# Moving one modulation piece of the feed-forward loop from ahead of the residual additions to behind the second one

## The chip, the cores and the metric

The kernel runs on one core of a Trainium2 chip. The metric is the time of one execution on the device in microseconds (us): the median of three runs, and less is better. Beside it there is one profiled execution, whose span and rows are read below.

The engines of the core are named as in the profile: PE (TensorE matmul), PEld (TensorE weight load), DVE (VectorE), ACT (ScalarE), POOL (GpSimd) and SP (SyncE, which here issues the loads of weights).

## The reference, cut to what matters

Two transformer blocks run one after the other on 1024 tokens of width 1024. The change lies in the feed-forward part of the first block, under which the kernel also computes the modulation vectors of the second block, since these depend only on the input `c`:

```python
h = _rmsnorm(x, norm_ffn[l])
gate, up = jnp.split(h @ w_gu[l], 2, axis=-1)          # 1024 x 2*2816
x = x + (jax.nn.silu(gate) * up) @ w_down[l]           # end of the first block
...
c_act = jax.nn.silu(c)                                 # one vector of 1024
shift, scale, gate = jnp.split(c_act @ ada_w[l] + ada_b[l], 3, axis=-1)   # for l = 0, 1
shift, scale = jnp.split(c_act @ kv_ada_w + kv_ada_b, 2, axis=-1)
```

Together the modulation is the product of one vector of 1024 with a matrix of 1024 x 8192. The kernel takes it in eight groups of 1024 columns, one group in each of eight passes of the loop, and each group in eight pieces of 128 rows.

## The kernel before, in words

**The hidden tiles.** The hidden width of 2816 is 22 tiles of 128. The first two are made before the loop, the others in ten steps `i` of two tiles: `i` = 0 stands alone and has no modulation, `i` = 1 to 8 are the passes of a hardware loop, each with one group of the modulation, and `i` = 9 stands alone behind it. A pass does three things on PE, in this order:

- `quad(i, 0, GATE_AT)`: the gate product of two new tiles, in seven products ("forms") of sums of weights with sums of activations (Strassen's scheme), 12 matmuls each;
- `down(i)`: the previous two hidden tiles (`act_hi`, `act_lo`) times the down weights, in eight output tiles `o` = 0 to 7, 12 matmuls each. Tile `o` goes to `pair(2 + o % 2)`, so only two PSUM pairs (banks 4 and 5, banks 6 and 7) take turns. From `o` = 2 on, tile `o` may start only when the residual addition of tile `o - 2` has read its pair;
- `quad(i, 1, UP_AT)`: the up product, seven forms again. The form with index 3 is the product's fourth.

The wait of `down(i)` in PE's queue is

```python
pe.wait_ge(ffn_res, 8 * i + (o - 1))
```

where `ffn_res` counts the residual additions, eight to a pass.

Each product is taken in a high and a low part (fp32r), which is why every piece gives matmuls at lines 691, 692 and 694 of the helper `product`.

**DVE** works through one program in order. In a pass that is `ada_add(i, 0)`, `gate_first`, `ada_add(i, 1)`, `gate_tiles` (additions of the gate product's forms, and at lines 3073 and 3077 the multiplication of `gated` by `rms3`), `ada_add(i, 2)`, and then the eight residual additions (line 3122, `xT` plus a PSUM pair), among which stand `gate_scale` (line 3082, behind `o` = 0 and `o` = 2) and pieces 3 to 6 of the modulation, behind `o` = 1, 3, 5 and 7. Piece 7 and `ada_turn` (a transpose and a reduction, lines 3005 and 3007) follow, and then `up_tiles`, which begins at line 3088 with reading bank 3.

**One piece of the modulation**, `ada_add(i, k)`, waits for its 128 x 1024 block of the matrix in `ada_raw[:, k % 2]` and adds its product with column `k` of `cact` to `ada_acc` (line 2998; the first piece, line 2995, writes it). Both of its large operands lie in SBUF.

**SP** issues every load in one queue. `load_ada(i, k)` (line 1275) waits for piece `k - 2`, since the pieces take turns in two buffers:

```python
sp.wait_ge(ada_summed, 8 * i + (k - 9))
```

Loads 0, 1 and 2 are queued ahead of `after_quad(i, GATE_AT, 2)`, load 3 behind it, and loads 4 to 7 behind `after_down(i, DOWN_AT, 4)`. These two issue halves of weight strips (line 1348), as soon as a form made from the half before is ready. What is queued behind load 7 is the first weight half of the next pass, which waits for the form with index 3 of the up product.

**POOL and ACT** make the forms of the weights: ACT writes the high part (line 2486), POOL the low part (line 1548) and the sums (lines 1559, 1561, 1564 and 1566), all from operands in SBUF. PE's form with index 3 of the up product needs POOL's chain 1548, 1564, 1566, 1548, of which the first starts when `down` has given back its last weights.

Of the kernel before, what the change touches and what calls it, by code (L numbers as in the profile page):

```python
# [132 lines left out]
def build(nc, dram, out):  # L133
    ctx = ExitStack()
    with ctx:
# [39 lines left out]
        def col(name, i=0, n=1):  # L175
# [7 lines left out]
        chk_stack, chk_khi, chk_klo = shared([("chk_stack", [P, HEADS, T], F32R), ("chk_khi", [P, HEADS, T], F32R),  # L183
                                              ("chk_klo", [P, HEADS, T], F32R)])
        _, p1, pt1 = shared([("mla_qkv", [P, 3 * HEADS, T], F32), ("p1", [P, 4, HALF], F32), ("pt1", [P, 4, HALF], F32)])
        h_hi, h_lo = sb("h_hi", [P, NK, T], F32R), sb("h_lo", [P, NK, T], F32R)

        mraw, kv_hi, kv_lo = shared([("mraw", [P, 6, T], F32), ("kv_hi", [P, T], F32R), ("kv_lo", [P, T], F32R)])
        _, swa_klo0, swa_bias, p3, pt3 = shared([("x_kept", [P, KEPT, T], F32), ("swa_klo0", [P, T], F32R),
                                                ("swa_bias", [P, SWA_HEADS, 2 * P], F32), ("p3", [P, 4, 2 * P], F32),  # L190
                                    ("pt3", [P, 4, 2 * P], F32)])
        fox_rows, = shared([("fox_rows", [P, QT, D], F32R)])
        _, memw_lo = shared([("w18", [P, 6, T], F32), ("memw_lo", [P, 2, 8, P], F32R)])
        _, p_lo_x = shared([("w20", [P, 6, T], F32), ("p_lo_x", [P, 2, T], F32R)])
        xT = sb("xT", [P, NK, T])
# [67 lines left out]
        def pair(p):  # L263

            return ps[:, 2 * p * HALF:2 * (p + 1) * HALF]
# [87 lines left out]
        def form_through(eng, i, p):  # L353
            eng.wait_ge(form_done, FORMS * i + p + 1)
# [2414 lines left out]
        def _(dve):  # L2769
# [220 lines left out]
            def ada_add(i, k):  # L2990

                r = k % 2
                dve.wait_ge(ada_loaded[r], 16 * (4 * i + (k // 2 - 3)))
                if k == 0:
                    dve.tensor_scalar(ada_acc[:, :], ada_raw[:, r, :], cact[:, 0:1], None, ALU.mult).then_inc(ada_summed, 1)
                else:
                    dve.wait_ge(ada_summed, 8 * i + (k - 8))
                    dve.scalar_tensor_tensor(out=ada_acc[:, :], in0=ada_raw[:, r, :], scalar=cact[:, k:k + 1],  # L2998
                                             in1=ada_acc[:, :], op0=ALU.mult, op1=ALU.add).then_inc(ada_summed, 1)

            def ada_turn(i):


                dve.wait_ge(ada_summed, 8 * i)
                dve.transpose(ada_turned, ada_acc[:, :]).then_inc(ada_turns, 1)
                dve.wait_ge(ada_turns, i)
                dve.tensor_reduce(ada_part[:, :], ada_turned.rearrange("p (b c) -> p b c", c=STREAM), AX.X, ALU.add)\
                   .then_inc(ada_parts, 1)

            def ada_columns(i):  # L3010
                dve.wait_ge(ada_cols, i)
                for q in range(P // STREAM):
                    r = slice(q * STREAM, (q + 1) * STREAM)
                    dve.tensor_tensor(adav[r, bass.ds(i * 8 - 8, 8)],
                                      bank(7, D // STREAM)[r, :].rearrange("p (t q) -> p q t", q=P // STREAM)[:, q, :],
                                      cols[r, bass.ds(i * 8 + (COLS["adab"] - 8), 8)], ALU.add).then_inc(ada_read, 1)
# [3 lines left out]
            def hidden_low(n, j, hi, lo):  # L3020

                dve.wait_ge(ffn_hi, HID * n + (j + 1))
                dve.tensor_tensor(lo[:, j, :], gated[:, j, :], rows(hi[:, j, :]), ALU.subtract).then_inc(ffn_lo, 1)
# [35 lines left out]
            def gate_first(i, at):  # L3059
                form_through(dve, i, at + 1)  # L3060
                dve.wait_ge(quad_first, 2 * i + 1)
                dve.wait_ge(ffn_lo, HID * i + HID)
                dve.tensor_tensor(gated[:, 0, t1], one_sum, bank(3), ALU.add).then_inc(quad_read, 1)

            def gate_tiles(i, at):
                two_products(i, 0, at)
                more_products(i, 0, at)
                dve.tensor_tensor(gated[:, 1, t2], three_sum, bank(2), ALU.add).then_inc(quad_read, 1)
                form_through(dve, i, at + 5)
                read_through(i, 0, 4)  # L3070
                dve.tensor_tensor(gated[:, 0, t2], two_sum, bank(3), ALU.add).then_inc(quad_read, 1)
                read_through(i, 0, 6)
                dve.tensor_tensor(gated[:, 0, :], gated[:, 0, :], rms3[:, :], ALU.mult).then_inc(ffn_gate, 1)
                form_through(dve, i, at + 6)
                dve.tensor_tensor(gated[:, 1, t1], three_sum, bank(1), ALU.add).then_inc(quad_read, 1)
                read_through(i, 0, 7)
                dve.tensor_tensor(gated[:, 1, :], gated[:, 1, :], rms3[:, :], ALU.mult).then_inc(ffn_gate, 1)

            def gate_scale(i, j):

                dve.wait_ge(ffn_silu, HID * i + (HID + j + 1))
                dve.tensor_tensor(gated[:, j, :], gated[:, j, :], rms3[:, :], ALU.mult).then_inc(ffn_mul, 1)

            def up_tiles(i, at):
                dve.wait_ge(ffn_mul, 2 * HID * i + 2 * HID)
                form_through(dve, i, at + 1)
                dve.wait_ge(quad_first, 2 * i + 2)
                dve.tensor_tensor(three_sum, one_sum, bank(3), ALU.add).then_inc(quad_read, 1)
                read_through(i, 1, 1)
                dve.tensor_tensor(gated[:, 0, t1], gated[:, 0, t1], three_sum, ALU.mult).then_inc(ffn_mul, 1)  # L3090
                two_products(i, 1, at)
                dve.wait_ge(ffn_mul, 2 * HID * i + 2 * HID + 1)
                more_products(i, 1, at)
                dve.tensor_tensor(one_sum, three_sum, bank(2), ALU.add).then_inc(quad_read, 1)
                read_through(i, 1, 5)
                dve.tensor_tensor(gated[:, 1, t2], gated[:, 1, t2], one_sum, ALU.mult).then_inc(ffn_mul, 1)
                form_through(dve, i, at + 5)
                dve.tensor_tensor(two_sum, two_sum, bank(3), ALU.add).then_inc(quad_read, 1)
                read_through(i, 1, 6)
                dve.tensor_tensor(gated[:, 0, t2], gated[:, 0, t2], two_sum, ALU.mult).then_inc(ffn_done, 1)  # L3100
                form_through(dve, i, at + 6)
                dve.tensor_tensor(three_sum, three_sum, bank(1), ALU.add).then_inc(quad_read, 1)
                read_through(i, 1, 7)
                dve.tensor_tensor(gated[:, 1, t1], gated[:, 1, t1], three_sum, ALU.mult).then_inc(ffn_done, 1)

            def ffn_pair(i, ada):
                if ada:
                    ada_add(i, 0)
                gate_first(i, GATE_AT)
                if ada:  # L3110
                    ada_add(i, 1)
                gate_tiles(i, GATE_AT)
                if ada:
                    ada_add(i, 2)
                for o in range(8):
                    if o % 2:
                        form_through(dve, i, DOWN_AT + o // 2)
                    else:
                        dve.wait_ge(ffn_tile, 4 * i + (o // 2 + 1))
                    if not isinstance(i, int):  # L3120
                        dve.wait_ge(ffn_res, 8 * i + (o - 7))
                    dve.tensor_tensor(xT[:, o, :], xT[:, o, :], pair(2 + o % 2), ALU.add).then_inc(ffn_res, 1)  # L3122
                    if o in (0, 2):
                        gate_scale(i, o // 2)
                    if ada and o % 2:
                        ada_add(i, 3 + o // 2)
                if ada:
                    ada_add(i, 7)
                    ada_turn(i)
                up_tiles(i, UP_AT)  # L3130
                if ada:
                    ada_columns(i)
                for j in range(HID):
                    hidden_low(i + 1, j, act_hi, act_lo)

            ffn_pair(0, False)
            with dve.Fori(1, FFN_ITERS - 1) as i:
                ffn_pair(i, True)
# [288 lines left out]
            for part, tok in enumerate(out_tokens):  # L3427
                for j in range(6 if part else NK):
                    i = NK * part + j
# [200 lines left out]
```

## Time and profile before

| | |
|---|---|
| median of 3 runs (lowest to highest) | 2430.15 us (2428.74 to 2436.74) |
| the profiled execution's own time | 2434.64 us |
| its span | 2432.8 us |
| PE busy | 2369.6 us, 97% |
| DVE busy | 1508.2 us, 62% |
| POOL busy | 1272.2 us, 52% |
| ACT busy | 833.1 us, 34% |
| mean granted clock of TensorE | 0.994 of full speed |

The profiled execution's time is its span and 1.8 us around it. It lies 4.5 us above the median of the runs. The eight passes of the loop lie between 812 and 1306 us of the span. Rows give the start and the duration in us from the span's start; a duration of a matmul is longer than the distance to the next, since matmuls are pipelined.

### The profile page before, as it was taken

The page shows a single profiled execution, that of the slowest core. Times are in us where ns is not written, and L with a number is a line of the kernel's source. Part 1 is how long each engine was busy: PE and PEld are TensorE (multiplying, and loading weights), DVE is VectorE, ACT ScalarE, POOL GpSimd, SP SyncE. Part 2 cuts the span into 40 slices and gives each one's busy share as a digit, 9 for nine tenths or more (in the row PEclk, how much of TensorE's full clock was granted, in tenths as well). Part 3 has the DMA queues.
Part 4 walks back from the last instruction along what each step waited for, and adds up shares of the span by engine and source line. Part 5 has one row for each costly group of instructions (what it writes and reads, how often), then busy time and mean ns, then how long its engine had stood idle before and what let it go on. Part 6 is the DMA issues. An engine that isn't in the chain of part 4 may idle for free.

```text
span 2432.8 us, 32824 instructions
## 1 busy us (share of the span) xinstructions
PE 2369.6 (97%) x11802; PEld 1967.0 (81%) x11810; DVE 1508.2 (62%) x1909; ACT 833.1 (34%) x1588; POOL 1272.2 (52%) x724
## 2 busy tenths in 40 slices
PE   7999999999999999999999999999999999999998
PEld 6887788888877888888888878878788787888887
DVE  6725555634577787877787678763754766045555
ACT  4211545612433222222222433231232333055663
POOL 4433964144144666666668344673746633465523
PEclk9999999999999999999999999999999999999999
DMA  6511000021011333333331111111221113100023
GB/s 213 160 44 44 1 1 27 10 113 44 18 40 48 113 121 121 121 121 121 121 121 65 48 44 44 56 66 52 69 82 56 56 65 130 52 27 19 27 104 131
DMA packets 67270, 177.31 MB, mean 73 GB/s; under 512 B 6846, under 2 KB 13760, under 8 KB 65112
## 3 DMA queue, kind: packets, MB, share of 16 engines
q1 hardware_dynamic: 58344, 148.58, 17.9%
q10 hardware_dynamic: 8816, 27.25, 3.2%
q8 instruction: 70, 1.15, 0.2%
q14 instruction: 40, 0.33, 0.0%
HBM read 160.04 MB, written 15.72 MB: 72 GB/s over the span
## 4 chain that ended last, share of the span: by engine, by line
PE 84%; DVE 7%; issue 4%; POOL 3%; ACT 2%; DMA 0%; SPq 0%; DVEq 0%; POOLq 0%; ACTq 0%
PE ps L691 22%; PE ps L692 22%; PE ps L694 22%; PE ps L843 6%; PE ps L821 5%; PE ps L831 3%; POOL split_lo L1597 1%; DVE h_lo L565 1%; DVE trail L3218 1%; PE ps L704 1%; PE ps L706 1%; PE ps L705 1%; PE ps L487 1%; DVE h_lo L568 1%; ACT p L971 0%
## 5 line engine op out<-in xcount | busy, mean ns | idle before, releaser
L691 PE MATMUL ps<-h_hi,split_hi 128*128 128x512 f32 (+1 forms) x1576 | 629.6, 399 | 20.5 <-DVE h_lo L568 13.8
L692 PE MATMUL ps<-h_lo,split_hi 128*128 128x512 f32 (+1 forms) x1576 | 613.5, 389 | 0.0
L694 PE MATMUL ps<-h_hi,split_lo 128*128 128x512 f32 (+1 forms) x1576 | 548.3, 389 | 0.0
L1473 POOL TENSOR_TENSOR split_hi<-raw,cf 128x1024 fp32r<-128x1024 f32 x70 | 136.9, 1955 | 496.9 <-PE ps L694 389.5
L691 PEld LDWEIGHTS ps<-h_hi,split_hi 128*128 128x128 f32 x1576 | 298.4, 189 | 81.3 <-issue 12.8
L694 PEld LDWEIGHTS ps<-h_hi,split_lo 128*128 128x128 f32 x1576 | 297.6, 189 | 62.0
L692 PEld LDWEIGHTS ps<-h_lo,split_hi 128*128 128x128 f32 x1576 | 298.5, 189 | 56.0 <-issue 1.2
L1548 POOL TENSOR_TENSOR split_lo<-raw,split_hi 128x512 fp32r<-128x512 f32 x144 | 231.2, 1624 | 201.5 <-ACT split_hi L2486 201.3
L1597 POOL TENSOR_TENSOR split_lo<-raw,split_hi 128x512 fp32r<-128x512 f32 x96 | 147.6, 1546 | 171.9 <-ACT split_hi L2644 171.7
L1475 POOL TENSOR_TENSOR split_lo<-raw,split_hi 128x1024 fp32r<-128x1024 f32 x70 | 195.3, 2789 | 5.5
L2486 ACT CAST split_hi<-raw 128x512 fp32r<-128x512 f32 x144 | 86.6, 622 | 287.0 <-PE ps L694 212.9
L879 DVE CUSTOM_DVE_ANT_0 p<-ps,swa_bias 128x256 f32<-128x256 f32 (+1 forms) x128 | 52.1, 407 | 154.2 <-PE ps L821 152.8
L979 ACT COPY pt<-ps 128x256 f32<-128x256 f32 (+3 forms) x216 | 79.8, 369 | 177.9 <-PE ps L831 177.0
L691 PE MATMUL ps<-act_hi,split_hi 128*128 128x512 f32 x320 | 125.5, 392 | 5.5 <-DVE xT L3122 5.5
L831 PE MATMUL ps<-cf,p 128*128 128x128 f32 x712 | 122.4, 277 | 7.6 <-ACT p L971 6.8
L692 PE MATMUL ps<-act_lo,split_hi 128*128 128x512 f32 x320 | 124.6, 390 | 0.0
L2644 ACT CAST split_hi<-raw 128x512 fp32r<-128x512 f32 x96 | 58.7, 621 | 162.2 <-PE ps L694 157.1
L831 PEld LDWEIGHTS ps<-cf,p 128*128 128x128 f32 x712 | 87.3, 145 | 29.0 <-ACT p L971 15.5
L3122 DVE TENSOR_TENSOR xT<-xT,ps 128x1024 f32<-128x1024 f32 x72 | 87.4, 1214 | 31.2 <-PE ps L694 31.2
L2998 DVE SCALAR_TENSOR_TENSOR ada_acc<-ada_raw,cact,ada_acc 128x1024 f32<-128x1024 f32 x56 | 103.6, 1850 | 0.8
L691 PE MATMUL ps<-p_hi,split_hi 128*128 128x512 f32 x256 | 100.1, 391 | 1.3 <-DVE p_lo L3202 1.3
L692 PE MATMUL ps<-y_lo,split_hi 128*128 128x512 f32 x256 | 99.6, 389 | 0.0
(447 smaller groups left out, 5136.4 us busy)
## 6 DMA issues: line engine op xcount, KB each, us to landing
raw<-in_strips SPq DMA_DIRECT2D x208, 256.0 KB, 2.7
raw<-in_strips SPq DMA_DIRECT2D x86, 512.0 KB, 3.5
ada_raw<-in_ada SPq DMA_DIRECT2D x64, 512.0 KB, 3.9
memw_raw<-in_mem_strips SPq DMA_DIRECT2D x8, 512.0 KB, 6.5
xT<-in_xT ACTq DMA_DIRECT2D x4, 1024.0 KB, 7.9
x_spill_d<-xT ACTq DMA_DIRECT2D x1, 3584.0 KB, 9.9
xT<-x_spill_d ACTq DMA_DIRECT2D x2, 1792.0 KB, 10.3
out_T<-out_sb SPq DMA_DIRECT2D x14, 256.0 KB, 2.3
```

Of the source, the lines that this page charges most:

```text
L691: pe.matmul(acc[:, a:b], w_hi, hi[:, a:b], start=first, stop=False)
L692: pe.matmul(acc[:, a:b], w_hi, lo[:, a:b], start=False, stop=False)
L694: mm = pe.matmul(acc[:, a:b], w_lo, hi[:, a:b], start=False, stop=last)
L821: mm = pe.matmul(at[:, lo:hi], q, k, start=j == 0, stop=j == len(group) - 1)
L831: mm = pe.transpose(bank(4 + b % 2, P, j * P), probs[:, (b0 + j) * P:(b0 + j + 1) * P], ident)
L843: mm = pe.matmul(o, a["pt"][:, w % 4, j * P:(j + 1) * P], unit["values"][b0 + j], start=b0 + j == 0, stop=b0 + j == nblk - 1)
L1473: pool.tensor_tensor(hi, raw[:, r, :], ones[:, 0:1].to_broadcast([P, D]), ALU.mult).then_inc(hi_split, 1)
L1475: pool.tensor_tensor(lo, raw[:, r, :], rows(hi), ALU.subtract).then_inc(split_ready[r], 1)
L1548: pool.tensor_tensor(form_tiles(split_lo, p), src, rows(form_tiles(split_hi, p)), ALU.subtract).then_inc(form_ready, 1)
L1597: pool.tensor_tensor(group_tiles(split_lo, p), src, rows(group_tiles(split_hi, p)), ALU.subtract).then_inc(form_ready, 1)
L2998: dve.scalar_tensor_tensor(out=ada_acc[:, :], in0=ada_raw[:, r, :], scalar=cact[:, k:k + 1], in1=ada_acc[:, :], op0=ALU.mult, op1=ALU.add) ...
L3122: dve.tensor_tensor(xT[:, o, :], xT[:, o, :], pair(2 + o % 2), ALU.add).then_inc(ffn_res, 1)
```

## The change

Piece 2 moves from ahead of the residual additions to behind the second of them (`o` = 1). Piece 3 goes from behind `o` = 1 to behind `o` = 3, piece 4 from `o` = 3 to `o` = 4, piece 5 stays behind `o` = 5, and piece 6 goes from `o` = 7 to `o` = 6. Piece 7 stays behind the last addition. The order of the loads in SP's queue and all waits are as they were.

```diff
+            ADA_AFTER = (1, 3, 4, 5, 6)
+
             def ffn_pair(i, ada):
                 if ada:
                     ada_add(i, 0)
                 gate_first(i, GATE_AT)
                 if ada:
                     ada_add(i, 1)
                 gate_tiles(i, GATE_AT)
-                if ada:
-                    ada_add(i, 2)
                 for o in range(8):
                     if o % 2:
                         form_through(dve, i, DOWN_AT + o // 2)
...
                     dve.tensor_tensor(xT[:, o, :], xT[:, o, :], pair(2 + o % 2), ALU.add).then_inc(ffn_res, 1)
                     if o in (0, 2):
                         gate_scale(i, o // 2)
-                    if ada and o % 2:
-                        ada_add(i, 3 + o // 2)
+                    if ada and o in ADA_AFTER:
+                        ada_add(i, 2 + ADA_AFTER.index(o))
                 if ada:
                     ada_add(i, 7)
                     ada_turn(i)
```

## Rows read from the trace of the kernel before

**Rows 1.** The page: an engine's busy time, and the chain that ended last, by engine.
```profile
PE 2369.6 (97%) x11802; PEld 1967.0 (81%) x11810; DVE 1508.2 (62%) x1909; ACT 833.1 (34%) x1588; POOL 1272.2 (52%) x724
...
PE 84%; DVE 7%; issue 4%; POOL 3%; ACT 2%; DMA 0%; SPq 0%; DVEq 0%; POOLq 0%; ACTq 0%
```

**Rows 2.** PE's waits from 812 to 1300 us: total, times, longest.
```profile
PE ps L691 <- DVE xT L3122: 5.5, 8, 0.8
```

**Rows 3.** PE's timeline: `down` of `i` = 0, its first matmul and the one behind it.
```profile
770.59 0.39 PE L691 MATMUL ps<-act_hi,split_hi 128*128 128x512 f32 x1
...
792.35 0.39 PE L691 MATMUL ps<-h_hi,split_hi 128*128 128x512 f32 x1
```

**Rows 4.** The same for `i` = 1, with its stall.
```profile
830.43 0.39 PE L691 MATMUL ps<-act_hi,split_hi 128*128 128x512 f32 x1
...
836.86 0.50 PE L691 MATMUL ps<-act_hi,split_hi 128*128 128x512 f32 x1 [0.83 <-DVE xT L3122]
...
853.36 0.39 PE L691 MATMUL ps<-h_hi,split_hi 128*128 128x512 f32 x1
```

**Rows 5.** The same for `i` = 4.
```profile
1013.83 0.39 PE L691 MATMUL ps<-act_hi,split_hi 128*128 128x512 f32 x1
...
1020.00 0.50 PE L691 MATMUL ps<-act_hi,split_hi 128*128 128x512 f32 x1 [0.57 <-DVE xT L3122]
...
1036.46 0.39 PE L691 MATMUL ps<-h_hi,split_hi 128*128 128x512 f32 x1
```

**Rows 6.** DVE's timeline in the pass `i` = 4.
```profile
1014.97 1.60 DVE L3077 TENSOR_TENSOR gated<-gated,rms 128x1024 f32<-128x1024 f32 x1
1016.50 2.32 DVE L2998 SCALAR_TENSOR_TENSOR ada_acc<-ada_raw,cact,ada_acc 128x1024 f32<-128x1024 f32 x1
1018.74 1.21 DVE L3122 TENSOR_TENSOR xT<-xT,ps 128x1024 f32<-128x1024 f32 x1
1019.87 1.21 DVE L3082 TENSOR_TENSOR gated<-gated,rms 128x1024 f32<-128x1024 f32 x1
1021.01 1.21 DVE L3122 TENSOR_TENSOR xT<-xT,ps 128x1024 f32<-128x1024 f32 x1
1022.14 1.27 DVE L2998 SCALAR_TENSOR_TENSOR ada_acc<-ada_raw,cact,ada_acc 128x1024 f32<-128x1024 f32 x1
...
1025.87 1.22 DVE L3122 TENSOR_TENSOR xT<-xT,ps 128x1024 f32<-128x1024 f32 x1 [0.20 <-PE ps L694]
1027.01 1.85 DVE L2998 SCALAR_TENSOR_TENSOR ada_acc<-ada_raw,cact,ada_acc 128x1024 f32<-128x1024 f32 x1
...
1032.45 1.84 DVE L2998 SCALAR_TENSOR_TENSOR ada_acc<-ada_raw,cact,ada_acc 128x1024 f32<-128x1024 f32 x1
...
1037.80 4.17 DVE L2998 SCALAR_TENSOR_TENSOR ada_acc<-ada_raw,cact,ada_acc 128x1024 f32<-128x1024 f32 x2
...
1044.42 0.68 DVE L3088 TENSOR_TENSOR quad_tmp<-quad_tmp,ps 128x512 f32<-128x512 f32 x1
```

**Rows 7.** SP's timeline: load 4 of `i` = 4.
```profile
1018.99 0.33 SPq L1275 DMA_DIRECT2D ada_raw<-in_ada  x1
```

**Rows 8.** Line 1275, all 64 loads of the modulation, from issue to landing.
```profile
DMA to landing us min/median/max: 3.4/3.9/5.6
```

**Rows 9.** POOL's timeline in the pass `i` = 4.
```profile
1015.45 2.28 POOL L1548 TENSOR_TENSOR split_lo<-raw,split_hi 128x512 fp32r<-128x512 f32 x1
1026.48 1.28 POOL L1548 TENSOR_TENSOR split_lo<-raw,split_hi 128x512 fp32r<-128x512 f32 x1 [8.75 <-ACT split_hi L2486]
...
1038.73 2.15 POOL L1564 TENSOR_TENSOR form_sums<-raw,form_sums 128x512 f32<-128x512 f32 x1
...
1043.08 1.29 POOL L1548 TENSOR_TENSOR split_lo<-form_sums,split_hi 128x512 fp32r<-128x512 f32 x1
```

**Rows 10.** TensorE at the up product's form with index 3: weight load, first matmul.
```profile
1044.50 0.19 PEld L691 LDWEIGHTS ps<-sum_hi,split_hi 128*128 128x128 f32 x1
...
1044.62 0.40 PE L691 MATMUL ps<-sum_hi,split_hi 128*128 128x512 f32 x1
```

## The prediction

> **What bounds the kernel now.** I read the page first. PE is busy 97% of the span, and the chain that ended last runs 84% through PE [rows 1]. So an edit on DVE is worth what it takes off PE's waits, and nothing else. Then I asked for PE's waits in the stretch of the eight loop passes. There is a single line: the first matmul of a product waited for the residual addition of line 3122 eight times, 5.5 us in all, 0.8 at most [rows 2]. It is once a pass. PE's timeline shows where: in the pass `i` = 4, `down` begins at 1013.83, and its third tile should begin two tiles of 2.72 later, at 1019.27. It begins at 1020.00, with 0.57 of idle time put down to line 3122 [rows 5]. That is `down`'s tile `o` = 2 waiting for residual addition 0.
>
> What the stall costs is more than the idle time in the row, since the matmuls restart slowly. The clean measure is a pass without a modulation: `down` of `i` = 0 takes 792.35 - 770.59 = 21.76 us, that is 96 matmuls at 0.2267 or 2.72 a tile [rows 3]. `down` of `i` = 1 takes 853.36 - 830.43 = 22.93, 1.17 more, where the row shows 0.83 idle [rows 4]. `down` of `i` = 4 takes 22.63, 0.87 more, where it shows 0.57 [rows 5]. So each stall costs its idle time and about 0.32. Eight of them: 5.5 + 8 x 0.32 = 8.1 us.
>
> Who makes addition 0 late is read in DVE's timeline: line 3077 runs from 1014.97, piece 2 of the modulation from 1016.50 for 2.32 us, and addition 0 only from 1018.74 [rows 6]. Its tile was finished at about 1016.84: a tile's addition can start 0.29 behind the end of its matmuls' issue, as addition 3 shows, which waited for PE and started at 1025.87, where tile 3 ended at 1020.00 + 2.86 + 2.72 = 1025.58 [rows 5, 6] (2.86 for the slow tile 2: 1036.46 less five tiles is 1022.86).
>
> **The change, part by part.** No instruction, wait or load is added or taken away; eight pieces are made in each pass as before. I work with times from the start of `down`, with no stall, so tile `o` ends at 2.72 x (`o` + 1) and can be added from 0.29 later; tile `o` + 2 needs the addition's end by 2.72 x (`o` + 2). Durations: an addition 1.21 with the next instruction 1.13 behind it, `gate_scale` the same, a piece 1.27 alone and 1.84 to 2.32 when POOL's instruction runs as it starts [rows 6, 9].
>
> *Piece 2 leaves.* Line 3077 is done at 1016.50 - 1013.83 = 2.67, addition 0 starts with its tile at 3.01 and ends at 4.22; PE wants it at 5.44. That wait goes, with 1.2 us to spare: -8.1 us. In the passes with a later line 3077, as `i` = 1, the bound is still the tile or close to it.
>
> *The rest of the chain.* `gate_scale` 0 from 4.14 to 5.35; POOL's instruction that could stand in its way ends at 1015.45 + 2.28, or 3.90 [rows 9]. If it were held like line 2998's 2.32, it would end by 6.5, addition 1 by 7.6, and PE wants that at 8.16: still hidden. Otherwise addition 1 runs 5.73 to 6.94, piece 2 to 8.13, addition 2 from 8.45 to 9.66 (wanted at 10.88), `gate_scale` 1 to 10.8, addition 3 from 11.17 to 12.38 (wanted at 13.60). Piece 3 starts at 12.30. POOL's line 1548 comes 0.90 behind the end of tile 3 (1026.48 against 1025.58), at 11.78, so piece 3 takes about 1.85, as piece 4 did at 1027.01. Addition 4 then runs from 14.1 to 15.3, wanted at 16.32: 1.0 to spare, the tightest place. Piece 4, now between additions 4 and 5, to 16.5; addition 5 from 16.61 to 17.8, wanted at 19.04. Additions 6 and 7 are waited for by nothing near: the up product uses banks 0 to 3. Cost on PE: 0.
>
> *The loads.* SP issued load 4 0.17 behind piece 2's end (1018.99 against 1018.82) [rows 6, 7]. A load now follows its releaser: load 4 at 8.3, load 5 at 14.3, load 6 at 16.6, load 7 at about 19.8. A load lands in 3.4 to 5.6, median 3.9 [rows 8]. Load 4 is there at 12.2, piece 4 wants it at 15.2: hidden. Load 5 lands at 17.7 to 19.9, and piece 5 wants it at 17.8: this is a new wait of 0 to 2.1 us on DVE, in front of additions 6 and 7 and pieces 6 and 7. Load 7 lands at 23.2 to 25.4, and piece 7 could start at about 23.2: again 0 to 2.2. Behind them are the turn and line 3088, which frees bank 3 for the sixth form of the up product, at 21.76 + 5 x 2.72 = 35.36. Before, line 3088 ran at 1044.42, which is 7.96 behind the end of `down`; now about 28 to 30 on this clock, 6.3 to 8.3 behind it. At least 5 us are left. Nothing of SP's queue is late: the next weight half behind load 7 waits for a form that is ready near 1044.4 [rows 9], some 10 us behind load 7's new place. Cost: 0.
>
> *POOL.* The tight place is elsewhere. POOL finishes the low part of the form with index 3 at 1043.08 + 1.29 = 1044.37 [rows 9], TensorE loads it at 1044.50 and starts at 1044.62 [rows 10], exactly where three forms of 8.16 behind 1036.46 put it. There is no slack at all. In that chain, line 1564 took 2.15 where 1.28 is the plain price, because piece 6 stood in front of it, and pieces 6 and 7 run from 1037.80 to 1041.97, beside lines 1564 and 1566 [rows 6, 9]. Now piece 6 starts around 20.7 to 22.2, near or ahead of the end of `down` (21.76), and piece 7 at 23.2 to 25.4. So POOL's four instructions from `down`'s end meet one or two pieces, where they met two: the form is ready 7.4 to 7.9 behind `down`'s end, against 7.91 before. Bounds of this term: -0.2 us (the 0.02 to 0.03 a pass by which TensorE is late there today, eight times) and, if a piece more than before came in between, 0.87 a pass (2.15 - 1.28), or 7.0. I take 0, since the piece that moved is moved out.
>
> A rule of the Trainium skill bears on this (SBUF — State Buffer, section "Who interferes with whom"): a VectorE instruction with two inputs in SBUF and a GpSimd instruction that reads SBUF exclude each other, and the later one blocks until the earlier is done. The rows agree in kind. By the rule a piece in the way can cost POOL its whole 1.27 instead of 0.87, and the give-back would be 10.2 us instead of 7.0.
>
> **Sum.** -8.1 + 0 + 0 + 0 = -8.1 us, against the profiled execution: 2434.64 - 8.1 = 2426.5. That execution is 4.5 above the median of the runs; on the median's scale 2430.15 - 8.1 = 2422.0, which is 0.33% less. What a measurement of this kernel can tell from no change is about 0.3%, or 7.3 us. The forecast lies just beyond that.
>
> **The rivals.**
>
> *One more piece in POOL's way.* The waits for loads 5 and 7 shift pieces 6 and 7 so that lines 1548, 1564 and 1566 meet more of them. For it: no slack at that form, and landing times differ from pass to pass. Against: there were two there before and at most two are left behind piece 5. At 0.87 in half of the passes 3.5 us come back (2425.5), in all of them 7.0 (2429).
>
> *The residual is late at another tile.* Addition 4 has only 1.0 to spare. If piece 3 took 2.32 and line 1548 came later yet, 0.5 would still be left. For a loss, DVE must be held over 1 us more than any row shows. Should every pass lose a stall of the old size again, the time is 2430.
>
> *Slower: the loads chain up.* Load 5 releases piece 5, that one load 7, that one piece 7, the turn and bank 3. With a landing time L, line 3088 ends at about 14.3 + 2L + 7.3, and it is wanted by 35.2: from L = 6.8 on PE waits, 2 us a pass for each us of L, and the gain is gone at 7.3. At L = 8, 8 x 2.4 - 8.1 = +11 us, 2441. Against it: the longest of 64 loads took 5.6 [rows 8], and now the loads are closer together only by pairs, 2.3 us (5 and 6).
>
> *The wait was not what held PE.* If the later of two causes were something else, nothing changes: 2430. But piece 2 is the only instruction between line 3077 and addition 0, and `i` = 0, without it, has no stall.
>
> **How the numbers follow.** The forecast 0.72, for faster by 7 to 9 us; since its centre is only 0.8 beyond the bound, 0.57 of it is faster and 0.15 within. One more piece in POOL's way 0.12, the residual late elsewhere or no effect 0.11: both within the bound. The chain of loads 0.05: slower. So faster 0.57, same 0.38, slower 0.05. The range goes from 2419.5 (8.1 and 0.2, with the lowest run's 1.4 under the median, and some 0.9 for a shift of the other places) to 2430 (nothing gained). The forecast's own range is 2420 to 2425.
>
> **What would show it.** In the changed kernel's trace the eight `down` parts take 21.76 each and the line of PE's waits for line 3122 is gone; addition 0 starts 3.0 behind `down`'s start; line 2998 shows waits for its load at pieces 5 and 7; line 3088 starts earlier than 7.96 behind `down`'s end, or close to it; the three forms in front of index 3 of the up product take 8.16. Wrong would be a new PE wait on line 1548 or 3088, or a stall at tile 6. The place where the sum is most exposed is the form with index 3.

## The result, and the profile after

| | before | changed |
|---|---|---|
| median | 2430.93 us (9 runs, 2428.74 to 2436.74) | 2424.40 us (9 runs, 2422.84 to 2428.05) |
| the profiled execution: time, span | 2434.64, 2432.8 us | 2422.84, 2421.0 us |
| PE busy | 2369.6 us, 97% | 2363.6 us, 98% |

The ratio is 0.9972, with a 95% interval of 0.9962 to 0.9982: faster by 0.28%, 6.5 us between the medians. The prediction was 2422.0 in a range of 2419.5 to 2430.0, and faster by 0.33%. Its most likely case was a gain of 7 to 9 us, and the measured one lies a little under that.

First the page of the changed kernel: PE's busy time, the chain by engine, and the first product of `down` with the idle time in front of it.

```profile
PE 2363.6 (98%) x11802; PEld 1965.5 (81%) x11810; DVE 1503.6 (62%) x1909; ACT 834.4 (34%) x1588; POOL 1272.9 (53%) x724
...
PE 86%; DVE 6%; issue 3%; POOL 3%; ACT 2%; DMA 0%; SPq 0%; POOLq 0%; ACTq 0%; DVEq 0%
...
L691 PE MATMUL ps<-act_hi,split_hi 128*128 128x512 f32 x320 | 124.5, 389 | 0.0
```

The last line is to be read with [rows 2]: 5.5 us of waits for line 3122 have become 0.0. In PE's timeline the `down` of `i` = 4 now has no gap:

```profile
1008.57 0.39 PE L691 MATMUL ps<-act_hi,split_hi 128*128 128x512 f32 x1
...
1030.33 0.39 PE L691 MATMUL ps<-h_hi,split_hi 128*128 128x512 f32 x1
```

That is 21.76 us, the figure of [rows 3], where it was 22.63 [rows 5]. All eight passes show 21.76, and from 812 to 1340 us PE has no wait that the view lists. From the first matmul of `down` in `i` = 0 to that in `i` = 9 the changed kernel takes 1328.01 - 768.49 = 559.52 us, and the kernel before took 1338.36 - 770.59 = 567.77. So 8.25 us left the loop between these two executions: 8.07 from the `down` parts and some 0.02 a pass from the two products between one `down` and the next.

DVE's timeline of the same pass answers to [rows 6]:

```profile
1009.49 2.09 DVE L3077 TENSOR_TENSOR gated<-gated,rms 128x1024 f32<-128x1024 f32 x1
1011.50 1.21 DVE L3122 TENSOR_TENSOR xT<-xT,ps 128x1024 f32<-128x1024 f32 x1
1012.63 1.21 DVE L3082 TENSOR_TENSOR gated<-gated,rms 128x1024 f32<-128x1024 f32 x1
1014.29 1.22 DVE L3122 TENSOR_TENSOR xT<-xT,ps 128x1024 f32<-128x1024 f32 x1 [0.45 <-PE ps L694]
1015.43 1.28 DVE L2998 SCALAR_TENSOR_TENSOR ada_acc<-ada_raw,cact,ada_acc 128x1024 f32<-128x1024 f32 x1
...
1022.64 1.21 DVE L3122 TENSOR_TENSOR xT<-xT,ps 128x1024 f32<-128x1024 f32 x1
...
1036.43 0.68 DVE L3088 TENSOR_TENSOR quad_tmp<-quad_tmp,ps 128x512 f32<-128x512 f32 x1
```

On the clock of the prediction (less 1008.57), addition 0 starts at 2.93, addition 1 at 5.72 (forecast 5.73), piece 2 at 6.86, addition 4 at 14.07 (forecast 14.1), line 3088 at 27.86, which is 6.1 behind the end of `down` in place of 7.96. Additions 1, 2 and 3 now wait for PE, which is the right way round.

### The profile page after: what moved, and what is told of

Its sections match the earlier page's. It is cut to its first block, busy times and chain, and to the rows that moved or that the text cites. A ratio compares the mean times of both kernels' runs of the same rounds, so it can differ in the third digit from the quotient of the medians.

```text
span 2421.0 us, 32824 instructions
## 1 busy us (share of the span) xinstructions
PE 2363.6 (98%) x11802; PEld 1965.5 (81%) x11810; DVE 1503.6 (62%) x1909; ACT 834.4 (34%) x1588; POOL 1272.9 (53%) x724
## 4 chain that ended last, share of the span: by engine, by line
PE 86%; DVE 6%; issue 3%; POOL 3%; ACT 2%; DMA 0%; SPq 0%; POOLq 0%; ACTq 0%; DVEq 0%
PE ps L691 23%; PE ps L692 22%; PE ps L694 22%; PE ps L843 6%; PE ps L821 5%; PE ps L831 3%; POOL split_lo L1597 1%; DVE trail L3218 1%; DVE h_lo L565 1%; PE ps L706 1%; PE ps L705 1%; PE ps L704 1%; PE ps L487 1%; DVE h_lo L568 1%; PE ps L519 0%
## 5 line engine op out<-in xcount | busy, mean ns | idle before, releaser
L3122 DVE TENSOR_TENSOR xT<-xT,ps 128x1024 f32<-128x1024 f32 x72 | 87.7, 1218 | 20.5 <-PE ps L694 19.1
L694 PE MATMUL ps<-act_hi,split_lo 128*128 128x512 f32 x320 | 98.5, 389 | 0.0
```

What stands on the lines that cost most here:

```text
L694: mm = pe.matmul(acc[:, a:b], w_lo, hi[:, a:b], start=False, stop=last)
```

## The experiments

Each was timed in five rounds against the kernel before on the same chip, unless it says otherwise. The medians of the kernel before in these sessions lay at 2429.6 to 2430.1.

### One part alone: only piece 2 moves (e1)

```diff
                 gate_tiles(i, GATE_AT)
-                if ada:
-                    ada_add(i, 2)
...
+                    if ada and o == 1:
+                        ada_add(i, 2)
                     if ada and o % 2:
                         ada_add(i, 3 + o // 2)
```

> One part of the change alone: piece 2 goes behind addition 1, where piece 3 also stays, and pieces 3 to 6 keep their places behind additions 1, 3, 5 and 7. If piece 2 ahead of addition 0 was the whole cause, addition 3 ends about 12.7 us behind the start of down (wanted at 13.60), all eight down parts take 21.76, and the time is that of the changed kernel, about 8 us under the kernel before. If the new places of the later pieces matter as well, a stall shows at tile 4 or 5 and the gain is smaller, by 8 us for each us of stall in a pass.

Measured: 2424.93 us, ratio 0.9980 (0.9971 to 0.9989). All eight `down` parts take 21.76, and the loop 559.69 us. Two pieces in a row behind addition 1 make DVE late for addition 3, but not late enough:

```profile
1016.48 2.60 DVE L2998 SCALAR_TENSOR_TENSOR ada_acc<-ada_raw,cact,ada_acc 128x1024 f32<-128x1024 f32 x2
1019.00 1.21 DVE L3120 TENSOR_TENSOR xT<-xT,ps 128x1024 f32<-128x1024 f32 x1
1020.13 1.22 DVE L3082 TENSOR_TENSOR gated<-gated,rms 128x1024 f32<-128x1024 f32 x1
1021.26 1.21 DVE L3120 TENSOR_TENSOR xT<-xT,ps 128x1024 f32<-128x1024 f32 x1
```

`down` began at 1009.62 there, so addition 3 ends at 12.85, and PE wants it at 13.60. The move of piece 2 is the whole of the gain but for some 0.2 us (the loop takes 559.69 here, 559.52 in the changed kernel). The new places of pieces 3, 4 and 6 are worth nothing that the time can show; they widen the margin.

### Piece 2 made short where it stood (e2)

```diff
+                    n = 8 if k == 2 else D
-                    dve.scalar_tensor_tensor(out=ada_acc[:, :], in0=ada_raw[:, r, :], scalar=cact[:, k:k + 1],
-                                             in1=ada_acc[:, :], ...
+                    dve.scalar_tensor_tensor(out=ada_acc[:, 0:n], in0=ada_raw[:, r, 0:n], scalar=cact[:, k:k + 1],
+                                             in1=ada_acc[:, 0:n], ...
```

> The order of the kernel before, but piece 2 works on 8 of its 1024 columns (its part of the modulation is left out). If the length of piece 2 ahead of addition 0 made the stall, the stall goes with it: down takes 21.76 in each pass and the time falls by about 8 us, as in the changed kernel. If something else kept addition 0 late (a semaphore, the load, the gate's activation), down still takes 22.4 to 22.9 and the time stays within 2 us of before.

Measured: 2424.80 us, ratio 0.9979 (0.9970 to 0.9988); seven `down` parts within 0.02 of 21.76 and one of 21.84; the loop 559.80. The kernel leaves out all but 8 columns of piece 2, so its output is wrong, and it serves for the time only. The order is that of the kernel before, and all waits are there, so it is the time that piece 2 takes, and no wait of its own, that held addition 0. That rules out the rival that the wait was not what held PE.

### Two pieces ahead of addition 0 (e3)

```diff
                     ada_add(i, 2)
+                    ada_add(i, 3)
...
-                    if ada and o % 2:
+                    if ada and o in (3, 5, 7):
                         ada_add(i, 3 + o // 2)
```

> The kernel before with pieces 2 and 3 both ahead of addition 0, pieces 4 to 6 as before. If PE waits for addition 0 alone, the stall grows by the price of a piece without POOL in its way, 1.20 us a pass, so down takes 23.6 to 24.1 and the time rises by 8 x 1.2 = 9.6 us over before, to about 2440. If the stall was hidden by something else, it rises by under 4 us.

Measured: 2441.60 us (6 runs), ratio 1.0053 (1.0037 to 1.0068): 12.0 over the kernel before, where 9.6 was expected. PE's waits in the loop, to be read beside [rows 2]:

```profile
PE ps L691 <- DVE xT L3123: 14.3, 8, 2.1
```

14.3 - 5.5 = 8.8 us more idle time, near the 9.6. But the loop takes 579.59 us, 11.8 more, so the expectation missed by 2.4 us on the time. Two of the passes are the cause: their `down` takes 25.8, and six take 23.4 to 24.0. In one of the two, PE's timeline behind the stall and the windows over it (engine busy times, then the granted clock, the DMA share and GB/s) show:

```profile
1148.56 0.63 PE L691 MATMUL ps<-act_hi,split_hi 128*128 128x512 f32 x1 [2.15 <-DVE xT L3123]
1148.98 0.63 PE L692 MATMUL ps<-act_lo,split_hi 128*128 128x512 f32 x1
1149.41 0.63 PE L691 MATMUL ps<-act_hi,split_hi 128*128 128x512 f32 x1
...
1152.30 0.39 PE L692 MATMUL ps<-act_lo,split_hi 128*128 128x512 f32 x1
```
```profile
1140.00:1146.00 6.00, 6.00 (x28) 4.97 (x27) 5.28 (x4) 2.64 (x3) 4.96 (x3) 1.00 0.38 124
1146.00:1152.00 6.00, 3.85 (x11) 2.67 (x10) 4.73 (x5) 0.00 (x0) 0.00 (x0) 0.73 0.70 218
```

Matmuls follow each other at 0.43 us in place of 0.23, TensorE's 1.2 GHz in place of 2.4, for some 3.4 us behind the stall. The two passes of 25.8 are the two with 2.15 of idle time; stalls of 1.29 to 1.99 in the other six did not bring it. (The last section shows that the length alone does not decide it.)

### Three pieces behind the last addition (e4)

```diff
-            ADA_AFTER = (1, 3, 4, 5, 6)
+            ADA_AFTER = (1, 3, 4, 7, 7)
```

(The loop that places the pieces is changed so that two can stand behind one addition.)

> The changed kernel, but pieces 5 and 6 stand behind addition 7 as well, so that pieces 5, 6 and 7 all run beside POOL's lines 1548, 1564 and 1566 that make the form with index 3 of the up product. If that form has no slack, as the prediction read it, one more piece in POOL's way makes it about 0.8 us late: the three forms ahead of it take some 8.9 to 9.1 in place of 8.16, PE waits for line 1548, and 8 x 0.8 = 6.5 us of the gain are given back. If the form has slack, or pieces do not block POOL, the time stays that of the changed kernel.

Measured: 2423.99 us (10 runs), ratio 0.9979 (0.9970 to 0.9989); the two products between the `down` parts of two passes take 38.34 to 38.36, in the kernel before 38.33 to 38.35, in the changed kernel 38.32. The expectation missed, and DVE's timeline says why:

```profile
1033.54 4.17 DVE L2998 SCALAR_TENSOR_TENSOR ada_acc<-ada_raw,cact,ada_acc 128x1024 f32<-128x1024 f32 x2
1039.15 2.04 DVE L2998 SCALAR_TENSOR_TENSOR ada_acc<-ada_raw,cact,ada_acc 128x1024 f32<-128x1024 f32 x1 [1.44 <-DMA ada_raw<-in_ada]
```

Piece 7 waited for its load, which piece 5 releases, until POOL's last instruction of the form, at line 1548, had begun at 1038.82. Only two pieces stood in POOL's way, and the form was ready 7.89 behind the end of `down`, as in the kernel before (7.91). The whole loop takes 560.33, 0.8 over the changed kernel; 0.6 of it lies behind the last pass, where PE waits once, 0.3 us, for DVE's line 3063. The run tells nothing of the form's slack, and another was needed.

### Two added products in POOL's way (e7)

```diff
+            def in_the_way(done):
+                dve.wait_ge(ada_summed, done)
+                dve.tensor_tensor(quad_tmp[:, 1:3, :]..., rms3[:, :], rms3[:, :], ALU.mult).then_inc(ada_summed, 1)
...
                 if ada:
+                    in_the_way(10 * i - 3)
                     ada_add(i, 7)
+                    in_the_way(10 * i - 1)
                     ada_turn(i)
```

(The counts of `ada_summed` in the other waits go by ten a pass.)

> The changed kernel with two added VectorE products of rms3 with itself, 128 x 1024, both operands in SBUF, results unused: one ahead of piece 7, one behind it. In the trace of e4 the form with index 3 of the up product was ready 29.65 us behind the start of down and PE did not wait, since piece 7 stood behind its load. Here nothing holds the added instructions: one stands in the way of line 1564, piece 7 in the way of 1566, the second in the way of the last 1548, so the form is ready near 31.05, 1.35 us late. If the form has no slack and pieces block POOL: the three forms ahead take about 9.5 in place of 8.16, PE waits for line 1548 in each pass, and the time rises by 8 x 1.35 = 10.8 us over the changed kernel. If POOL is not blocked or the form has slack: no rise in PE, though DVE is 2.4 us a pass busier.

Measured: 2437.19 us (7 runs), ratio 1.0028 (1.0016 to 1.0039). The two products take 39.67 to 39.69 in place of 38.32, so 1.35 a pass as expected, and the loop 570.37, 10.85 over the changed kernel. The first added product on DVE, POOL's timeline in the pass `i` = 4, PE's wait behind it, and the waits in the loop:

```profile
1037.17 2.31 DVE L3110 TENSOR_TENSOR quad_tmp<-rms 128x1024 f32<-128x1024 f32 x1
```
```profile
1037.11 1.29 POOL L1548 TENSOR_TENSOR split_lo<-form_sums,split_hi 128x512 fp32r<-128x512 f32 x1
1038.48 2.15 POOL L1564 TENSOR_TENSOR form_sums<-raw,form_sums 128x512 f32<-128x512 f32 x1
1040.71 2.16 POOL L1566 TENSOR_TENSOR raw<-raw,form_sums 128x512 f32<-128x512 f32 x1
1042.82 2.26 POOL L1548 TENSOR_TENSOR split_lo<-form_sums,split_hi 128x512 fp32r<-128x512 f32 x1
```
```profile
1045.21 0.49 PE L691 MATMUL ps<-sum_hi,split_hi 128*128 128x512 f32 x1 [1.05 <-POOL split_lo L1548]
```
```profile
PE ps L691 <- POOL split_lo L1548: 8.5, 8, 1.1
```

The form was ready at 1042.82 + 2.26 = 1045.08, and `down` had begun at 1014.08: 31.00, against 31.05 expected. Three POOL instructions in a row cost 0.86 to 0.97 more than their 1.29. So the prediction's rival has its mechanism: DVE instructions in POOL's way delay this form, and PE waits for it. The reading "no slack at all" holds for the kernel before, where the form was ready 7.91 behind the end of `down`. In the changed kernel it is ready at 7.44 (7.42 to 7.53 over the eight passes), and here at 31.00 - 21.76 = 9.24: 1.80 later, of which PE lost 1.35. So the change itself left a slack of some 0.45 us in front of this form, and an instruction in the way costs time only beyond that.

### Later loads (e5)

```diff
-                    sp.wait_ge(ada_summed, 8 * i + (k - 9))
+                    sp.wait_ge(ada_summed, 8 * i + (k - (8 if k > 4 else 9)))
```

> The changed kernel, but loads 5, 6 and 7 of the modulation wait for the piece just before them in place of the one before that, so each is issued later and DVE waits some 3.5 us in front of each of pieces 5, 6 and 7. By the sum of the prediction line 3088 then ends near 33 to 35 us behind the start of down, and bank 3 is wanted at 35.2: DVE idles about 8 us more in each pass, and PE loses nothing or next to nothing (0 to 2 us in all). If waits for the loads reach PE through DVE's queue, each pass loses what DVE waits and the time rises by 10 us or more above the changed kernel.

Measured: 2433.25 us (11 runs), ratio 1.0014 (1.0005 to 1.0023). The loop takes 568.81, 9.29 over the changed kernel, in place of 0 to 2. Its waits and DVE's timeline (DVE waited 2.3 to 2.6 us for each of the three loads, not 3.5):

```profile
PE ps L691 <- DVE quad_tmp L3088: 6.8, 8, 0.9
```
```profile
1032.31 2.04 DVE L2998 SCALAR_TENSOR_TENSOR ada_acc<-ada_raw,cact,ada_acc 128x1024 f32<-128x1024 f32 x1 [2.32 <-DMA ada_raw<-in_ada]
...
1043.48 1.86 DVE L2998 SCALAR_TENSOR_TENSOR ada_acc<-ada_raw,cact,ada_acc 128x1024 f32<-128x1024 f32 x1 [2.42 <-DMA ada_raw<-in_ada]
...
1047.80 0.68 DVE L3088 TENSOR_TENSOR quad_tmp<-quad_tmp,ps 128x512 f32<-128x512 f32 x1
```

`down` began at 1012.15, so line 3088 ended at 36.33, 1.1 behind the 35.2 at which the prediction said it was wanted, and the pass lost 1.16. The place and the price of the chain of loads were right; my estimate of where this edit would put line 3088 (33 to 35) was 1.3 short at its upper end.

### The changed kernel again (e6), and two more traces of the kernel before (e8, e9)

> The changed kernel itself once more, beside the kernel before on the same chip. By the trace 8.25 us are saved inside the loop in each execution, so the ratio should lie at 0.9966 (0.9960 to 0.9972). If some of that is lost behind the loop in most executions, it stays at 0.9972 to 0.9980.

Measured: 2425.05 us (11 runs), ratio 0.9982 (0.9973 to 0.9991), loop 559.52 again to the hundredth. So the changed loop did not vary between its two traces, but the difference of the medians is 5.1 us, not 8.25.

> The kernel before, unchanged, for a second trace. The trace on record lost 8.07 us in its eight down parts, five stalls of 1.12 to 1.17 and three of 0.67 to 0.87, while the medians differ by only 5 to 7 us. If the size of the stall depends on which engine came first in a pass, and other executions have more of the small ones, this trace shows a sum of 6 to 7 us. If the sum is 8.1 again, the rest of the gain is lost outside the loop or in its scatter.

> The same as e8, a third trace of the kernel before: a sum of 6 to 7 us in the down parts if the stalls vary from execution to execution, 8.1 if they do not.

Measured, one execution each, unchanged code: 2430.62 and 2436.66 us. What the eight `down` parts of the kernel before took over 8 x 21.76, and the three parts of each span:

| kernel | `down` parts over 174.08 | to the start of `down` at `i` = 0 | loop | behind it |
|---|---|---|---|---|
| before, on record | 8.07 | 770.59 | 567.77 | 1094.44 |
| before (e8) | 6.37 | 769.98 | 566.06 | 1092.76 |
| before (e9) | 7.20 | 772.76 | 566.88 | 1095.16 |
| changed, on record | 0.0 | 768.49 | 559.52 | 1092.99 |
| changed (e6) | 0.0 | 770.21 | 559.52 | 1092.77 |

The size of the stall varies from pass to pass and execution to execution. In e8 a `down` began at 1073.84, and DVE was through with line 3077 2.35 us later, where the long stalls have 2.93:

```profile
1074.77 1.51 DVE L3077 TENSOR_TENSOR gated<-gated,rms 128x1024 f32<-128x1024 f32 x1
1076.19 2.32 DVE L2998 SCALAR_TENSOR_TENSOR ada_acc<-ada_raw,cact,ada_acc 128x1024 f32<-128x1024 f32 x1
1078.44 1.21 DVE L3122 TENSOR_TENSOR xT<-xT,ps 128x1024 f32<-128x1024 f32 x1
```

That pass stalled PE for 0.25 in place of 0.83. In all 24 passes of the three traces the loss follows the end of line 3077: 0.39 us where it ended 2.27 behind the start of `down`, 1.17 where it ended 3.01 behind it. What made line 3077 late is argued and not tested: DVE's lines 3073 and 3077 and POOL's line 1548 fell differently against each other, and line 3073 took 1.90 there, and 1.22 to 2.33 in other passes. On average over the three traces the stalls cost 7.2 us.

## Why the prediction was right, point by point

**The stall and its cause.** Right. PE waited for addition 0 and for nothing else; it is gone in every pass (e1, e2 and the changed kernel), and it grows when another piece is put ahead (e3).

**-8.1 us for it.** Right for the execution it was read from (8.07), too large for the kernel: this term was mis-sized by taking one profiled execution for all. Three traces give 8.1, 6.4 and 7.2, so 7.2 with the 0.2 of the up product added is 7.4 us. The profiled execution was slower than the median of the runs by 4 us, but that was no sign of its stalls: e9 was 2 us slower still, and its stalls cost 7.2. Against the forecast's own 7 to 9 us, the measured 6.5 and 5.1 both lie below: the median of 2424.40 lies well inside the stated range, but the gain was put too high.

**What is left between 7.4 and the measured 6.5 and 5.1.** Open. The medians of e1, e2 and e4, whose `down` parts have no stall either (0.1 us in all in e2), lie 4.7 to 5.7 under the kernel before, so these four runs put the gain nearer 5 than 6.5. The loop of the changed kernel takes 559.52 in both its traces. The part ahead of it differs among the five traces of the table by 4.3 us and the part behind it by 2.4, with the same code, so a difference of 1 to 2 us between medians can't be placed. TensorE's granted clock goes with a part of this scatter. Behind the loop, and before the last 12 us of the span, it stood at its lower level, 1.2 GHz, for 20.5 us in five of the eleven traces (the kernel before on record, e9, e1, e2, e7), and the part behind the loop took 1094.2 to 1096.9 there. In four (the changed kernel on record, e8, e3, e5) it was 17.1 us with 1092.8 to 1093.1, and in two (e4, e6) 13.7 us with 1091.2 and 1092.8. All eleven run the same code there, and traces of the kernel before stand in two of the groups. 7.4 us would be a ratio of 0.9970, inside the first interval, and at or just outside the edge of those of e1, e2, e4 and e6.

**The rest of the chain at no cost.** Right, to within 0.1 us for each instruction from addition 1 to addition 4. The tightest place was addition 4, at 14.07.

**The loads.** Right that they cost nothing; the expected waits of DVE, up to 2.1 us in front of piece 5 and piece 7, were nearly absent. In the waits of the changed kernel they are

```profile
DVE ada_acc L2998 <- DMA ada_raw<-in_ada: 0.4, 2, 0.2
```

The loads landed sooner than [rows 8] has it, 3.5 us in the median for 3.9:

```profile
DMA to landing us min/median/max: 3.4/3.5/6.0
```

On the clock of the prediction load 5 then lands at 17.8, just when piece 5 wants it. That the chain of loads would reach PE through bank 3 once line 3088 ends behind 35.2 was shown by e5.

**POOL.** The estimate was 7.4 to 7.9 behind `down`'s end for the form with index 3. In the changed kernel it is the last 1548 of

```profile
1031.59 1.30 POOL L1548 TENSOR_TENSOR split_lo<-form_sums,split_hi 128x512 fp32r<-128x512 f32 x1
1032.97 2.16 POOL L1564 TENSOR_TENSOR form_sums<-raw,form_sums 128x512 f32<-128x512 f32 x1
1035.21 1.31 POOL L1566 TENSOR_TENSOR raw<-raw,form_sums 128x512 f32<-128x512 f32 x1
1036.46 1.31 POOL L1548 TENSOR_TENSOR split_lo<-form_sums,split_hi 128x512 fp32r<-128x512 f32 x1
```

ready at 1037.77, 7.44 behind 1030.33, where it was 7.91, so some 0.45 of slack is new. One piece (7) is left in its way, at line 1564. PE was 0.02 to 0.03 a pass late at this form before and is not now; that is the gain on top of the stall. The rival that a piece more would come in its way did not occur, but e7 shows its mechanism: two instructions more cost 10.85 us.

**The Trainium skill's rule** (SBUF — State Buffer, section "Who interferes with whom"), by which the later of two such instructions (one of DVE with two inputs in SBUF, one of POOL that reads SBUF) blocks until the earlier is done, agrees in kind with e7. A block cost POOL 0.86 to 0.97 us there, and not the whole 1.27 that I had priced by the page. The rows suggest why: the first added product ended at 1037.17 + 2.31 = 1039.48, so its 1.27 of work began near 1038.21, and line 1564 started 0.27 later, when at most 1.00 of it was left (an estimate from these rows).

## What to carry to other kernels

When an in-order engine both frees the accumulators of TensorE and does work that nobody waits for, put the first freeing operation ahead of all such work: here a piece of 2.3 us (1.27 when POOL does not hold it) in front of the first of eight additions cost 0.4 to 1.2 us a pass, and behind the second it cost nothing. Lay the moved work out on a clock that starts with the consumer, with the time at which each addition is wanted; that sheet also finds the next tight place, here a weight form made by POOL, whose instructions DVE's can block. Read the size of a stall from more than one trace before betting on a few tenths of a per cent: here the same code lost 0.39 to 1.17 us a pass, 6.4 to 8.1 us in all.

## What the runs showed of the hardware that was not expected

TensorE's clock fell to 1.2 GHz behind two of the eight stalls of e3, the two of 2.15 us, and not behind the six of 1.29 to 1.99. The matmuls behind it came at 0.43 us for some 3.4 us, the granted clock of the window around it was 0.73, and the pass lost 4.04 - 2.15 = 1.9 us beyond its idle time. So such a stall cost nearly twice its length.

The length of the idle time does not decide it alone. In the same trace, behind the loop, the clock fell behind an idle time of 1.97 us and did not fall behind one of 2.66. PE's timeline at both places, and the windows over them:

```profile
1633.01 0.49 PE L691 MATMUL ps<-pool_sums,split_hi 128*128 128x512 f32 x1 [1.97 <-POOL split_lo L1597]
1633.35 0.52 PE L692 MATMUL ps<-pool_sums,split_hi 128*128 128x512 f32 x1
1633.67 0.63 PE L694 MATMUL ps<-pool_sums,split_lo 128*128 128x512 f32 x1
...
1760.70 0.50 PE L691 MATMUL ps<-pool_sums,split_hi 128*128 128x512 f32 x1 [2.66 <-DVE gates L3347]
1761.04 0.39 PE L692 MATMUL ps<-pool_sums,split_hi 128*128 128x512 f32 x1
```
```profile
1633.50:1636.90 3.40, 3.40 (x10) 2.65 (x9) 2.39 (x2) 0.49 (x1) 3.40 (x3) 0.50 0.52 154
1758.00:1768.00 10.00, 7.34 (x33) 5.93 (x32) 9.79 (x11) 1.96 (x4) 6.39 (x5) 1.00 0.35 105
```

At one and the same place of the program, an idle time of 2.35 us near 1409 was followed by a fall in e1 (granted clock 0.89 from 1405 to 1420), and one of 2.34 in e6 was not (1.00 over the same stretch). What decides it is open: no run here tests it.
